# Twelve rotary turns done by transfers between partitions instead of by TensorE matmuls, in a conformer, expert and sparse-attention kernel on one core

## The reference, cut to what matters

```python
x = x + 0.5 * swiglu(rmsnorm(x, g_ffn1), w1_gate, w1_up, w1_down)
p = rmsnorm(x, g_mix) @ w_in
qa, ka, va, qi, ki, wi, cq, ckv, kr = split(p)
qa, ka = apply_rope(qa), apply_rope(ka)        # 8 heads of 64, one key head
qi, ki = apply_rope(qi), apply_rope(ki)        # 16 index heads of 64, one key head
out_a = dsa_sparse_attention(qa, ka, va, qi, ki, wi)   # the 128 best keys by the index scores
out_b = mla_attention(cq, ckv, kr, ...)        # 8 heads, 64 plain + 32 rotary rows
x = x + concat(out_a, out_b) @ w_out
x = x + 0.5 * swiglu(rmsnorm(x, g_ffn2), w2_gate, w2_up, w2_down)

def apply_rope(x):                             # halves x1, x2 of each head
    return concat(x1 * cos - x2 * sin, x1 * sin + x2 * cos)
```

## Time and profile before

| | |
|---|---|
| time, median of 3 runs | 1966.82 us |
| the profiled execution | 1966.62 us, its span 1964.6 us |
| TensorE matmul busy | 1880.4 us, 96% of the span |
| VectorE / ScalarE / GpSimd busy | 1110.6 / 673.7 / 354.2 us |
| mean rate of the DMA engines | 247 GB/s |
| granted TensorE clock, mean | 0.997 |

### The profile page before, as it was taken

The page is one execution under the profiler, slowest core; times in us unless marked ns, Lnnn a source line. Parts: engine busy times, 40 slices in busy tenths (PEclk is TensorE's granted clock), DMA queues, the critical chain, the costliest instruction groups (busy, mean ns, idle before and its releaser), DMA issues. The chain is left out here.

```text
span 1964.6 us, 26526 instructions
## 1 busy us (share of the span) xinstructions
PE 1880.4 (96%) x9569; PEld 1343.8 (68%) x9570; DVE 1110.6 (57%) x1680; ACT 673.7 (34%) x1030; POOL 354.2 (18%) x430
## 2 busy tenths in 40 slices
PE   8999999998997789998899999999999899999998
PEld 7888888785332233333588887887665589999886
DVE  4998993444111111111634336965687638777897
ACT  4234435432000000000422224562336746444566
POOL 2023233201221112222011000012255500010100
PEclk9999999999999999999999999999999999999999
DMA  6489999997999999999466534677980065666565
GB/s 208 149 291 291 252 326 237 301 381 290 424 426 427 426 427 425 393 426 423 163 214 214 155 96 140 193 181 184 234 192 12 1 148 155 181 181 183 174 197 171
DMA packets 202680, 485.84 MB, mean 247 GB/s; under 512 B 34892, under 2 KB 113153, under 8 KB 177370
## 3 DMA queue, kind: packets, MB, share of 16 engines
q1 hardware_dynamic: 171802, 384.24, 54.5%
q0 software_dynamic: 30768, 100.31, 20.0%
q10 hardware_dynamic: 16, 0.00, 0.0%
HBM read 475.17 MB, written 111.67 MB: 299 GB/s over the span
## 5 line engine op out<-in xcount | busy, mean ns | idle before, releaser
L561 PE MATMUL psum<-h_hi,w_hi 128*128 128x512 f32 (+1 forms) x1240 | 449.8, 363 | 6.2 <-DVE h_lo L1043 1.9
L563 PE MATMUL psum<-h_hi,w_lo 128*128 128x512 f32 (+1 forms) x1240 | 445.3, 359 | 0.0
L562 PE MATMUL psum<-h_lo,w_hi 128*128 128x512 f32 (+1 forms) x1240 | 445.1, 359 | 0.0
L556 DVE TENSOR_TENSOR w_lo<-w_raw,w_hi 128x1024 fp32r<-128x1024 f32 (+1 forms) x144 | 178.2, 1238 | 296.3 <-ACT w_hi L551 296.2
L551 ACT ACTIVATE w_hi<-w_raw 128x1024 fp32r<-128x1024 f32 (+1 forms) x144 | 151.7, 1053 | 502.0 <-PE psum L563 454.3
L561 PEld LDWEIGHTS psum<-h_hi,w_hi 128*128 128x128 f32 x1240 | 234.2, 189 | 46.0 <-issue 7.1
L562 PEld LDWEIGHTS psum<-h_lo,w_hi 128*128 128x128 f32 x1240 | 234.3, 189 | 35.3 <-issue 1.4
L563 PEld LDWEIGHTS psum<-h_hi,w_lo 128*128 128x128 f32 x1240 | 234.2, 189 | 34.9
L1409 PE MATMUL psum<-arena,w_raw 128*64 128x512 f32 x800 | 181.7, 596 | 13.5 <-DMA arena<-in_w_expert_up_dram 12.6
L1544 ACT ACTIVATE w_raw<-psum 128x256 f32<-128x256 f32 x36 | 13.8, 384 | 464.1 <-PE psum L1409 464.1
L1071 DVE SCALAR_TENSOR_TENSOR arena<-arena,vec 128x512 f32<-128x512 f32 x240 | 162.6, 748 | 1.0 <-ACT arena L898 1.0
(11 more groups left out here) (394 smaller groups left out, 3197.8 us busy)
## 6 DMA issues: line engine op xcount, KB each, us to landing
arena<-in_w_expert_gate_dram SPq DMA_DIRECT2D x44, 1024.0 KB, 19.4
arena<-in_w_expert_up_dram SPq DMA_DIRECT2D x44, 1024.0 KB, 23.4
arena<-in_w_expert_down_dram SPq DMA_DIRECT2D x22, 2048.0 KB, 28.8
weight_terms<-in_w_down_dram POOLq DMA_DIRECT2D x60, 512.0 KB, 7.9
w_raw<-in_w_in_dram SPq DMA_DIRECT2D x44, 512.0 KB, 8.6
expert_down_third<-in_w_expert_down_dram SPq DMA_DIRECT2D x10, 2048.0 KB
expert_input<-in_w_expert_gate_dram SPq DMA_DIRECT2D x20, 1024.0 KB, 22.4
expert_input<-in_w_expert_up_dram SPq DMA_DIRECT2D x20, 1024.0 KB, 26.3
```

What stands on the lines that cost most here:

```text
L556: eng.tensor_tensor(wlo[:, s, :, 0:n], raw[:, slot, :, 0:n], whi[:, s, :, 0:n].bitcast(F32), ALU.subtract).then_inc(w_lo, 1)
L561: eng.matmul(o, w_h, x_h, start=first, stop=False)
L562: eng.matmul(o, w_h, x_l, start=False, stop=False)
L563: return eng.matmul(o, w_l, x_h, start=False, stop=last)
```

## The change

The constant matrix is no longer used for the twelve query tiles. `turn_rows` on ScalarE's queue waits for the read of a group and issues four transfers of 32 partitions by 2048 columns (256 KB each) that exchange the halves of all heads of the group's four tiles: after the group of chunks 4 to 7 (at c = 8, before the split of chunk 10), after that of 8 to 11 (at c = 12), and after that of 16 to 19, before ScalarE's copies of the key product. Index tiles are turned into the place where the attention queries come later; VectorE therefore waits for all ten turns before it reads the last group. Each landing is waited for by the sines and, for the attention tiles, by GpSimd's cosines, which waited for TensorE before. VectorE's product becomes a `scalar_tensor_tensor` of the turned tile, a new sign column and the sines, all in SBUF. TensorE loses twelve matmuls and its waits for the sines, and waits for the read of the last group instead. The lot of seven weight sums after the sixth cosine is given up and the one before the first is cut to five; groups 5 and 6 of the first gate and up issue four each, and six instead of five are left for the end.

```diff
-STEPS_IN_FIRST, STEPS_PER_GROUP, GROUPS_WITH_STEPS = 108, 4, 5
-STEPS_IN_MIX = {0: 7, 6: 7, 10: 8, 13: 5}
+STEPS_IN_FIRST, STEPS_PER_GROUP, GROUPS_WITH_STEPS = 108, 4, 7
+STEPS_IN_MIX = {0: 5, 10: 8, 13: 5}
...
+        turned_keys = [qa[:, i, :] for i in range(4)]
+        rows_at = [ar3[:, 18688:20736], ar3[:, 20736:22784], ar3[:, 0:2048]]
+        turn_in = x_in[0:3]
+
+        def turn_rows(act_eng, i):
+
+            group_read(act_eng, G_MIX + (1, 2, 4)[i])
+            if i == 1:
+                act_eng.wait_ge(mx["rope"], R_QI + 4)
+            to, source = rows_at[2] if i < 2 else after_groups[:, 3584:5632], rows_at[i]
+            for b in (32, 0, 96, 64):
+                act_eng.dma_start(to[b:b + 32], source[b ^ 32:(b ^ 32) + 32]).then_inc(turn_in[i], 16)
...
                 if b == 3:
                     pe.wait_ge(mx["rope"], R_QI + q + 1)
-                    pe.wait_ge(mx["rot_read"], R_QI + (4 if q < 4 else 8))
...
-                if c == 8:
-                    rotate_rows(range(2, 6))
-                if c == 12:
-                    rotate_rows(range(6, 10))
...
-            rotate_rows(range(R_QA, len(ropes)))
...
-            pe.wait_ge(mx["rot_read"], len(ropes))
+            group_read(pe, G_MIX + 4)
...
             for c in range(4, 20):
+                if c in (8, 12):
+                    turn_rows(act, c // 4 - 2)
...
+            turn_rows(act, 2)
             act.wait_ge(mx["acc"], 2 * N_IDX)
...
+            def signed_sine(r, part):
+                dve.wait_ge(turn_in[(r - R_QI) // 4], 80)
+                dve.scalar_tensor_tensor(out=part, in0=part, scalar=sign, in1=sin_of["A"], op0=ALU.mult,
+                                         op1=ALU.mult).then_inc(mx["rot_read"], 1)
+
             def sine(r):
                 kind = ropes[r][1]
+                if r >= R_QI:
+                    signed_sine(r, turned_keys[(r - R_QI) % 4])
+                    return
...
                 for r in range(R_QA, len(ropes)):
-                    dve.wait_ge(mx["rot"], r + 1)
-                    dve.tensor_tensor(sine_of_query[r - R_QA], psum[:, rot_bank[r], :], sin_of["A"], ALU.mult).then_inc(
-                        mx["rot_read"], 1)
+                    signed_sine(r, sine_of_query[r - R_QA])
...
                 if c % 4 == 3:
+                    if c == 19:
+                        dve.wait_ge(mx["rope"], R_QA)
                     read_group(c // 4)
...
             for r in range(R_QA, len(ropes)):
-                pool.wait_ge(mx["rot"], r + 1)
+                pool.wait_ge(turn_in[2], 80)
                 pool.tensor_tensor(cos_at(r), ropes[r][0], cos_of[ropes[r][1]], ALU.mult).then_inc(mx["cos"], 1)
```

More of the change, by code:

```diff
@@ L104 @@
 K_HALF = 1220
+K_SIGN = 1221
 K_CA = 1224
@@ L135, in constants @@
     c[:, K_HALF] = p // CAP
+    c[:, K_SIGN] = np.where(p % HDA < HDA // 2, -1, 1)
     def angles(dim):
@@ L2642, in program @@
         pe_rows = slice(NOPE, HQ)
-        rot_bank = [4, 5] + [0, 1, 2, 3] + [4, 5, 6, 7] + [4, 5, 6, 7]
+        rot_bank = [4, 5]
         rot_group = [0] * 2 + [1] * 4 + [2] * 4 + [4] * 4
@@ L3039, in dve_mix @@
             split_lo(dve, C_MIX, 5)
+            sign = const[:, K_SIGN:K_SIGN + 1]
+            def signed_sine(r, part):
+                dve.wait_ge(turn_in[(r - R_QI) // 4], 80)
+                dve.scalar_tensor_tensor(out=part, in0=part, scalar=sign, in1=sin_of["A"], op0=ALU.mult,
+                                         op1=ALU.mult).then_inc(mx["rot_read"], 1)
             def sine(r):
                 kind = ropes[r][1]
+                if r >= R_QI:
+                    signed_sine(r, turned_keys[(r - R_QI) % 4])
+                    return
                 dve.wait_ge(mx["rot"], r + 1)
-                if r >= 3:
-                    dve.wait_ge(mx["rope"], r - 2)
                 dve.tensor_tensor(pr[:, r % 3, :], psum[:, rot_bank[r], :], sin_of[kind], ALU.mult).then_inc(
@@ L3052, in rotated @@
                 if r:
-                    dve.tensor_tensor(src, cos_at(r), pr[:, r % 3, :], ALU.add).then_inc(mx["rope"], 1)
+                    part = turned_keys[(r - R_QI) % 4] if r >= R_QI else pr[:, r % 3, :]
+                    dve.tensor_tensor(src, cos_at(r), part, ALU.add).then_inc(mx["rope"], 1)
                     return
```

## The result

| | before | after |
|---|---|---|
| time, median | 1966.97 us (6 runs) | 1977.08 us (6 runs, 1975.3 to 1978.5) |
| ratio, 95% interval | 1 | 1.0051 [1.0038, 1.0064] |
| profiled execution, span | 1964.6 us | 1975.1 us |
| granted TensorE clock, mean | 0.997 | 0.992 |

The change costs 10.1 us. The forecast was 3.1, with an upper end of 1975.0.

A forecast was written before the change was run, and what follows sets the result against it. TensorE, busy 96%, was taken as the bound up to the last chunk, then VectorE up to the first score. Terms -1.7 - 1.7 + 5.7 + 0.8 = +3.1 us on the median 1966.82 gave 1969.9, range 1962.0 to 1975.0.

The forecast's parts named there:

- What bounds the stage: Up to the last chunk a microsecond saved on TensorE counts; from there to the first score only one on VectorE.
- VectorE's lateness: At the queries' turn, VectorE finishes the sines at 1472.1 against 1466.37, 5.7 us later, delaying the first score as much.
- clock at the first score: TensorE idles some 8.5 us before the first score, so its clock falls once; 0 to 1.7 us, taken as 0.8.
- A gain of 1.7 us, at most 3.4: At each of the two index turns, the first score pair after the turn starts 1.7 us sooner.
- The landing is at 1466.0: Queries' turn: transfers land at 1465.4 or 1467.2 beside the sums, taken as 1466.0, stalling VectorE by 2.1 us.
- Taking turns, four sines need 6.1 us: Queries' turn: VectorE's four sines and GpSimd's cosine products exclude each other; 6.1 us with VectorE first, otherwise 7.4.
- Rival (a): Queries' turn: no exclusion on VectorE, sines 2.0 us late, idle costs 0.3; -1.1 us in all, 1965.7; chance 0.22.
- (b): All turns: transfers go at 0.42 MB/us and there is no exclusion; -5.0 us, 1961.8; chance 0.15.
- Sums moved, ScalarE's copies: Moved sums are free with 0.9 us of cover in gate and up; ScalarE's later copies at the queries' turn cost nothing.
- rival (c): Queries' turn: GpSimd goes first after landing at 1467.2, VectorE 8.2 late, clock 1.7, turns 1.2 each; +7.5, 1974.3; chance 0.18.
- The main case's own range, 1967 to 1973: Range around the likeliest 1969.9 (chance 0.38), with turns 1.1 to 3.4 each and VectorE 5.4 to 7.0.
- The freed lot: Giving up seven sums between the index turns frees the queue, so the second turn also gains 1.7; nothing waited for them.

The follow-up runs named there:

- the run with the other order: The changed kernel with each turn's four transfers issued to destination quarters 32, 96, 0, 64 instead of 32, 0, 96, 64; 1977.15 us, ratio 1.0052.

## Why the prediction was wrong, point by point

- **What bounds the stage**: right. A wait of VectorE ahead of the sines went one to one into the first score (leaves 8.8 later, score 8.7 later).
- **The miss in the terms of the sum**: +9.9 by the distances against +3.1. Index turns -0.3 instead of -3.4 (3.1 of the miss), VectorE's lateness 8.5 instead of 5.7 (2.8), clock at the first score 1.7 instead of 0.8 (0.9).
- **"A gain of 1.7 us, at most 3.4" for each index turn**: mis-sized. The landing came 6.9 us after the first issue, not 5.9: the issue took 3.15 us (one of 1.23 among them), not 2.4, and a turn held the engines for 4.6 us (57.4% of 8 us) where 4.2 had been taken from the small swaps. The pairs came 0.65 and 0.75 us earlier. The Trainium skill, page "SBUF — State Buffer", section "Door 1: The DMA port swizzle", has 32 partitions reach half of the ports, about 218 GB/s at most. The estimate of 1.1 that was drawn from it was nearer than 1.7, and the trace agrees with the figure: all of a turn's 1.05 MB moved from 1358 to 1363, 0.21 MB/us.
- **A term that was missing**: the new wait of 2.7 us was taken to cost only its length. The clock fell behind it at the second turn and ate nearly all of the 1.4. The sum had a term for the clock at the first score and none here; the row it rested on showed a wait of 3.87 us. Of the 3.1 us by which both turns together missed, some 1.8 are the size (-1.6 instead of -3.4 with the clock held) and 1.3 the clock.
- **"The landing is at 1466.0"**: this step failed. It was 1469.4, or 12.0 us after the first issue instead of 8.7. The step let every queue move one packet in a round: a sum's, a load's and a turned row's, eight rounds of 0.80 or 1.02 us. The trace shows no such rounds. While the sums ran, their packets and SyncE's went nearly in turn (90 and 107 in 3 us) and the turn's stood still, for 4.0 us after the first issue; then its 192 packets, twelve for each engine and not eight, took 8 us beside SyncE's loads. Among those are 576 KB of constants, issued 1.8 and 1.3 us ahead of the turn. The step let one load packet in each round stand for all of them, where 540 went beside the turn's 192 (1461 to 1470). With sums and constants both away the lateness is gone. VectorE's shorter sines (5.77 instead of 6.1) took a little of it back, which leaves the 2.8 of the sum.
- **"Taking turns, four sines need 6.1 us"**: right, 5.77, and 2.74 without GpSimd. Rival (a), which said there is no exclusion, is refuted, and with it (b). The Trainium skill, page "SBUF — State Buffer", section "Who interferes with whom", says this of any VectorE instruction with two SBUF inputs beside a GpSimd one that reads SBUF. The trace agrees with it for this one: 1.75 against 0.75 us.
- **The clock at the first score, 0.8 of 0 to 1.7**: it took the whole 1.7, and 2.6 to 3.2 in kernels whose wait was 4.5 to 10.1 us. That VectorE paces these units hid none of it.
- **Sums moved, ScalarE's copies**: right. No wait in the gate and up; the value product waits 1.8 us for ScalarE (1.9 forecast) and nobody waits for that.
- **The main case's own range, 1967 to 1973**: its terms add up to 1966.2 at the lower end (turns 3.4 each, VectorE 5.4, clock 0.8), not 1967. Nothing else rests on it.
- **The freed lot**: the text said that nothing waited for it and that it only paid for a free queue. True of the kernel before; with the turns by transfers the same lot costs 4.4 us.

The sum with measured terms: -0.3 + 8.5 + 1.7 = +9.9. What happened is nearest to rival (c) (VectorE 8.8 late instead of 8.2, clock 1.7), but with index turns that bring 0.3 instead of 2.4; that is why the time lies 2 us above the upper end. It is only partly (c)'s mechanism: VectorE reached that lateness by a later landing, not by GpSimd taking the first turn.

## What to carry to other kernels

When work moves from a matmul to a transfer, price the transfer beside everything that is queued at that moment on all queues. Look for its first packet as well as its landing, since here it did not share with the sums but stood behind them. Look at who else starts on its landing: two engines released by one event can exclude each other. Ahead of the engine that sets the pace, place the wait behind other work; here moving the sines 22 steps back, ordering GpSimd behind them and filling the idle time gave back the whole loss, and no more. A new idle gap of TensorE, even of 2.7 us, has a second price in the clock behind it: read the granted clock in the windows after it before you count the gain.

## What the runs showed of the hardware

- Granted clock after a gap: 0.57 behind a wait of 2.67 us, where the wait of 2.76 at the first turn of the same execution left it at 1.00; in the run with the other order it fell behind both (2.46 and 2.38 us). Price of one such fall 1.1 to 1.3 us. Fillers in the gap kept it at 1.00 in the profile of each kernel that had them. What decides between two waits of the same length is open.
- At the first score the price does not go by the length of the wait: 3.2 us after 4.5, 2.9 after 7.1, 2.9 after 10.1, 1.7 after 10.2 and 1.7 after 11.0. Why is open.
- 256 KB exchanges between quarters of 32 partitions: 4 issues of 0.51 to 1.23 us each, landings 2.9 us at the least; 6.9 us for four when the queues are half empty, 11.1 to 12.0 beside sums and constants.
- Behind GpSimd's adding transfers, ScalarE's queue moved its first packet 3.6 to 4.2 us after the first issue in eleven executions; with the queues half empty 1.0 and 1.2 us in the changed kernel. SyncE's packets kept moving all the while.
- Two transfers side by side that write different halves of the partitions (32 and 96) bring a turn 0.3 us forward, 3% of the 8.9 us to the first pair. The Trainium skill, page "SBUF — State Buffer", section "Door 1: The DMA port swizzle", puts 0 to 63 and 64 to 127 on different ports, which fits; no run tells ports from other causes.
